# Splitting each weight unit's transfer by partitions: rows 120 to 127 apart from rows 0 to 119

## What is computed

```python
def reference(x, p, w_in_even, ..., mlp_w1_2, mlp_w2_2):
    x = first_block(x, p, w_in_even, ...)     # gated short conv beside a gated delta rule, then HGRN2;
                                              # each with w_in, w_out, layer norm, gate and w_pl
    return second_block(x, c_2, ada_w_2, ...) # conformer conv + MLP, block attention + MLP
# second_block, for i in range(DEPTH):
#   mod = silu(c) @ ada_w[i] + ada_b[i]                      (six vectors that scale and shift)
#   y = conformer_conv(h, ...)  or  moba_attention(h, ...)   ;  x = x + g1 * y
#   x = x + g2 * (square(relu(h @ mlp_w1[i])) @ mlp_w2[i])
```

## Time and profile before

| | |
|---|---|
| time, median of 3 runs | 1291.71 us (1291.06 to 1295.96) |
| the profiled execution's own time | 1290.79 us |
| its span, first to last instruction | 1289.0 us |
| TensorE busy | 1265.1 us, 98% of the span |
| VectorE busy | 971.0 us, 75% |
| ScalarE busy | 746.8 us, 58% |
| granted TensorE clock, mean | 0.997 |
| moved by the 16 DMA engines | 247.51 MB, 192 GB/s |

### The profile page before, as it was taken

The page is one execution under the profiler, slowest core; times in us unless marked ns, Lnnn a source line. Parts: engine busy times, 40 slices in busy tenths (PEclk is TensorE's granted clock), DMA queues, the critical chain, the costliest instruction groups (busy, mean ns, idle before and its releaser), DMA issues.

```text
span 1289.0 us, 29783 instructions
## 1 busy us (share of the span) xinstructions
PE 1265.1 (98%) x12990; PEld 1152.2 (89%) x12990; DVE 971.0 (75%) x1533; ACT 746.8 (58%) x1019; POOL 28.3 (2%) x66
## 2 busy tenths in 40 slices
PE   9999998999999999999999989999999999999998
PEld 9999998899899999998988769888889998988887
DVE  6878767656778888887767987898787765886543
ACT  6776353464765565554464156777346885778431
POOL 0000000000000000000000000000000000000000
PEclk9999999999999999999999999999999999999999
DMA  8553445446476565554332335688874432675552
GB/s 313 187 177 123 166 164 199 167 166 216 164 262 219 216 222 197 199 218 175 131 131 84 115 139 190 218 318 320 312 286 146 164 132 99 234 259 206 190 189 66
DMA packets 34946, 247.51 MB, mean 192 GB/s; under 512 B 3904, under 2 KB 3904, under 8 KB 5504
## 3 DMA queue, kind: packets, MB, share of 16 engines
q1 hardware_dynamic: 29104, 204.96, 43.4%
q0 software_dynamic: 5712, 40.63, 8.7%
HBM read 244.53 MB, written 1.05 MB: 191 GB/s over the span
## 4 chain that ended last, share of the span: by engine, by line
PE 87%; DVE 7%; ACT 4%; issue 2%; POOL 0%; DVEq 0%; ACTq 0%; POOLq 0%
PE PS L510 17%; PE PS L426 10%; PE PS L427 9%; PE PS L428 9%; PE PS L511 9%; PE PS L527 5%; DVE WL L660 2%; PE PS L442 2%; ACT WH L627 2%; PE PS L443 2%; PE PS L444 2%; PE PS L1119 2%; PE PS L509 1%; PE PS L1051 1%; DVE BIG L305 1%
## 5 line engine op out<-in xcount | busy, mean ns | idle before, releaser
L660 DVE TENSOR_TENSOR WL<-RAW,WH 128x2048 fp32r<-128x2048 f32 x166 | 379.9, 2290 | 105.8 <-ACT WH L627 102.3
L627 ACT ACTIVATE WH<-RAW 128x2048 fp32r<-128x2048 f32 x166 | 316.9, 1909 | 147.3 <-PE PS L511 66.5
L426 PE MATMUL PS<-XW,WH 128*128 128x256 f32 x928 | 270.8, 292 | 0.0
L427 PE MATMUL PS<-XW,WH 128*128 128x256 f32 x928 | 262.4, 283 | 3.0 <-issue 3.0
L428 PE MATMUL PS<-XW,WL 128*128 128x256 f32 x928 | 262.2, 283 | 0.0
L427 PEld LDWEIGHTS PS<-XW,WH 128*128 128x128 f32 x928 | 177.7, 192 | 3.3 <-issue 3.2
L426 PEld LDWEIGHTS PS<-XW,WH 128*128 128x128 f32 x928 | 177.2, 191 | 3.6 <-issue 1.1
L428 PEld LDWEIGHTS PS<-XW,WL 128*128 128x128 f32 x928 | 177.5, 191 | 0.0
L510 PE MATMUL PS<-XW,WH 128*128 128x512 f32 x392 | 141.0, 398 | 0.3
L510 PE MATMUL PS<-YW,WH 128*128 128x512 f32 x368 | 129.9, 395 | 0.0
L305 DVE SCALAR_TENSOR_TENSOR BIG<-BIG,C 128x256 f32<-128x256 f32 (+2 forms) x232 | 103.0, 504 | 13.8 <-ACT BIG L1485 7.4
(11 more groups left out here) (436 smaller groups left out, 2558.8 us busy)
## 6 DMA issues: line engine op xcount, KB each, us to landing
RAW<-wst SPq DMA_DIRECT2D x191, 1024.0 KB, 4.8
BIG<-wad POOLq DMA_DIRECT2D x38, 1024.0 KB, 5.1
X<-xT SPq DMA_DIRECT2D x2, 512.0 KB, 5.1
RAW<-wst SPq DMA_DIRECT2D x2, 512.0 KB, 6.5
outT<-X SPq DMA_DIRECT2D x4, 256.0 KB, 4.3
K<-cst SPq DMA_DIRECT2D x1, 608.0 KB
CB<-crow SPq DMA_DIRECT2D x1, 512.0 KB
BIG<-pT POOLq DMA_DIRECT2D x2, 256.0 KB, 4.8
```

The lines of the kernel that those rows point to most:

```text
L426: pe.matmul(o, h, hl[0][:, k0 + k, :], start=(k == 0), stop=False)
L427: pe.matmul(o, h, hl[1][:, k0 + k, :], start=False, stop=False)
L627: ac.activation(WH[p % NS][:, :], RAW[u % NR][:, :], ACT.Copy).then_inc(S.hi.tick(p), 1)
L660: ve.tensor_tensor(WL[p % NS][:, :], RAW[u % NR][:, :], WH[p % NS][:, :].bitcast(f32), ALU.subtract).then_inc(S.lo.tick(p), 1)
```

## The change

```diff
-                sp.dma_start(RAW[u % NR][:, :], wst[u if plan else 0]).then_inc(S.raw[u % NR].tick(u, by=16), 16)
+                w = wst[u if plan else 0]
+                sp.dma_start(RAW[u % NR][120:128, :], w[120:128]).then_inc(S.raw[u % NR].tick("last rows", u, by=16), 16)
+                sp.dma_start(RAW[u % NR][0:120, :], w[0:120]).then_inc(S.raw[u % NR].tick(u, by=16), 16)
```

## The result

The changed kernel takes 1417.33 us (median of 4 runs, 1411.58 to 1420.14), the kernel before on the same chips 1292.85 us (4 runs, 1291.06 to 1295.96). The ratio is 1.095, with a 95% interval of 1.0927 to 1.0973. It is 9.5% slower. The prediction was 1292.0 us, with 1297.8 as its upper end and a chance of 0.05 on slower. It was wrong.

The account below looks back on a forecast made before the run. TensorE, busy 1265.1 of 1289.0 us, was taken as the bound. Issues 0, six L627 landings 0, start 0 to 0.3, stretched landings the odd 0.1: +0.3 us on 1291.71 gives 1292.0 us, range 1289.6 to 1297.8.

Parts of the forecast that it names:

- (a): One more issue on SP per unit, ahead of the 120 partitions: their landing moves by 0.33 us in the steady part.
- (b): Sharing a unit over DMA engines: 15 engines take eight packets, eight take one more, at 0.35 us a packet.
- The bounds: Later landing of each unit: +0.33 us if only the issue counts, +0.68 us if the two transfers queue; +0.5 us taken.
- The covers: Slack between late weight landings and TensorE: 0.67 us at the start, 0.76 and 1.05 us at L627; all six exceed 0.68.
- The load, 78.5%: Busiest stretch: nine packets for eight make 46.3 x 9/8 + 26.4 = 78.5% on the busiest DMA engines, so they don't fill up.
- The nine landings without slack: ACT waited for a landing nine times among 178 weight instructions, 24.4 us in all; every other landing was already there.
- The 120 partitions use half of the engines: Rival, slower: 120 partitions go to 8 engines, landings 2.8 us later, busiest load 119%; +30 us, 1322 us, chance 0.05.
- busy for the same 1265 us: Expected profile after the change: TensorE's busy time stays at 1265 us, with an idle time of 24 us.
- All nine: Rival, no measurable change at its upper end: all nine later landings reach TensorE; +6.1 us, 1297.8 us, chance 0.07.
- the freed engine: Rival, faster: the DMA engine left without weights ends TensorE's unexplained stalls and L660 waits; 8.7 us less, 1283.0 us, chance 0.03.
- The signs named: Failure marks: L660 waits over 4 us, ACT's landing waits many more than nine or 2 us longer, unexplained TensorE stalls changing.

Follow-up runs that it names:

- cols: Every unit moved as two transfers of all 128 partitions, columns 0 to 1023 and 1024 to 2047, against the kernel before: 1295.17 us, ratio 1.0018.
- ramp_only: The split into 8 and 120 partitions for units 1 to 5 only, all others whole, against the kernel before: 1304.87 us, ratio 1.0087.

## Why the prediction was wrong, by its own steps

**(a), the issue, was right.** The issues take 0.27 and 0.33 us in the median, and cols with just as many of them costs 0.2%.

**(b), the sharing out, failed, by its price.** The count was right: 15 engines and 8, one packet and eight. The records agree, since 191 x (128 + 23) + 1600 = 30441 is the page's number. The step that failed is "0.35 us a packet" taken from the earlier trace rows and carried over unchanged to another set of partitions. It is 0.59 us for the 120 and, with a full queue, 1.20 us for the last eight. The bounds, +0.33 to +0.68 us a landing, took the 120 partitions to land as fast as 128 (at the lower end) or by that price (at the upper), so neither held the truth: +2.6 us for a lone pair (7.43 against 4.81), and with a full queue 3.1 us more for each unit.

Here a rule had been at hand. The Trainium skill, "SBUF — State Buffer", section "Door 1: The DMA port swizzle", says that the partitions decide which of 16 ports a transfer reaches. Counting ports would still have said 16 for 0 to 119. What matters is which engines are behind one port at the same time, and that is nowhere in the rows of before, where all large transfers have 128 partitions.

**The covers.** With +0.68 us they might have held; no run tried that. With +3 us none of 0.67 to 1.05 us does. The start shows it alone: 7.0 us of waits for L641 in ramp_only.

**The load, 78.5%.** "They don't fill up" failed through the same price: with 5.85 for 2.78 us a unit the term is 124%, and measured were 0.91 of the engines' time in a stage grown from 233 to 291 us. Over 100% it would have turned the forecast by itself. As a forecast of the time it is too low, as the other cuts show, because it holds POOL's 26.4% fixed. The nine landings without slack were the wrong thing to look at: ACT waited 49 times at L627, 26 of the times in the MLP's window, where before there was no such wait at all.

**The rivals.** "The 120 partitions use half of the engines" had the side, a price near the true one (16 packets for 8, a load of 119%) and the place, but the wrong cause, as 135 records show, and a chance of 0.05. Its 1322 us were too little, since it counted a stretch of 100 us of a stage that lasts 233, and left out the start, the delta rule and TensorE's clock. The clock lies, by the estimate above, behind most of the 44.7 us of longer products; the prediction had "busy for the same 1265 us" and no term for it. "All nine", at most +6.1 us, and "the freed engine", which was to be faster, did not occur.

**The signs named** were right: the step on sharing out was to be wrong if ACT's waits were many more than nine, the covers if L660 cost over 4 us. It is 52 and 45.1 us. And the forecast was to fail if an unexplained stall grew, as it did from 6.5 to 30.8 us; for this part the cause stays open.

No version here beats the kernel before. The only cut that nearly keeps its time, at +0.2%, is the one by columns, where each transfer goes to all 128 partitions.

## What to carry to other kernels

The price of a packet belongs to the set of partitions that it is shared out over, and not to its size. If a change alters how many partitions a transfer touches, price it anew, by timing it alone and back to back, before any count of engines or slack is trusted. And if transfers get dearer, look first at the busiest stretch: where share x new price passes 100%, the stage takes at least that product, whatever its slack was. Take it as a lower bound: at 97% a stage was already 17% longer here, where POOL's transfers had got dearer too. Then add what an engine pays that has to stand still.

## What the runs showed of the hardware

- 120 of 128 partitions land later than all 128 (7.03 against 4.81 us), and so do 112 (5.50) and 96 (5.12); 64 take nearly as long as 128 (4.55 and 4.68). Back to back: 4.85 us for 120, 2.78 for 128.
- Eight neighbouring rows of 8 KB take 1.37 us of full queue, half of what a whole unit of 1 MB takes (2.78).
- Eight rows of 32 KB take 6.32 us into neighbouring partitions and 3.83 us into partitions four apart.
- Transfers to all 128 partitions get dearer beside cut ones: POOL's packets have a median of 0.31 us before and 0.47 us in the changed kernel.
- Two halves by partitions cost 5.1 us, two halves by columns 2.97.
- Out of SBUF 120 partitions are slower than 128 too: 5.77 against 3.90 us.
- 28 MB of transfers from HBM to HBM for which nobody waits cost a kernel 1.1%: TensorE's unexplained stillness went from 6.5 to 18.7 us.
- Of the 128 us lost, 44.7 are longer products; by the mean granted clock, 0.967 against 0.997, some 43 of them are the lower clock, in stages where TensorE had to wait. A wait costs more than its length.
